# A trunk layer on eight cores: attention weights summed before the ones product, one bias added from PSUM, a revised planner, some Toeplitz pieces on ScalarE

## The reference

```python
x = x + 0.5 * swiglu_ffn(rmsnorm(x, ffn1_norm), ffn1_w_in, ffn1_w_out)      # D 1024, D_FF 2816
h = rmsnorm(x, mix_norm)
u_conv, q, k, v, g_conv, g_attn = jnp.split(h @ w_in, idx, axis=-1)
a = conformer_conv(u_conv, ...)        # GLU, causal depthwise width 31, layernorm, silu, projection
b = sliding_window_gqa(q, k, v, ...)   # 16 query heads, 4 key heads of 64, window 128
merged = jax.nn.sigmoid(g_conv) * a + jax.nn.sigmoid(g_attn) * b
x = x + merged @ w_out
x = x + 0.5 * swiglu_ffn(rmsnorm(x, ffn2_norm), ffn2_w_in, ffn2_w_out)

# inside the attention, per block of 128 queries and its two key blocks
s = s + bias[None, None]
m = jnp.maximum(jnp.max(s, axis=-1, keepdims=True), sink)
p = jnp.exp(s - m)
p = p / (jnp.sum(p, axis=-1, keepdims=True) + jnp.exp(sink - m))
o = jnp.einsum("bnhgqk,bnkhd->bnqhgd", p, vw)
```

## Time and profile before

| what | value |
|---|---|
| median of three executions | 3040.81 us |
| the profiled execution's own time | 3036.41 us |
| its span, slowest core (core 7) | 3034.8 us |
| spans of all cores | 3018.6 to 3034.8 us |
| PE busy, core 7 | 2973.1 us, 98% |
| DVE, ACT, POOL busy, core 7 | 1236.7, 836.3, 743.4 us |

### The profile page before, as it was taken

One profiled execution on the slowest core, in us unless ns is written; L12 is line 12 of the kernel. 1 busy time (PEld: TensorE's weight loads), 2 busy tenths in 40 slices (PEclk: granted clock), 3 DMA queues, 4 the chain that ended last, 5 costly groups with the idle time before them and its releaser, 6 DMA issues.

```text
span 3034.8 us, 41593 instructions; the slowest of 8 cores (3018.6 to 3034.8 us)
## 1 busy us (share of the span) xinstructions
PE 2973.1 (98%) x14660; PEld 1340.0 (44%) x14660; DVE 1236.7 (41%) x1700; ACT 836.3 (28%) x1482; POOL 743.4 (24%) x655
## 2 busy tenths in 40 slices
PE   6999999999999999999899999999999999999998
PEld 3444444444444454454334434434444444444443
DVE  4323345423344223757444454553323333223333
ACT  4111123211123222414666656642211111111110
POOL 3100012100003434293465555563000000000000
PEclk9999999999999999999999999999999999999999
DMA  7514249513148677967934545689442139332102
GB/s 181 92 23 70 35 115 239 105 21 60 21 100 218 133 181 174 221 121 231 179 81 138 143 140 149 161 194 237 138 90 42 21 69 228 87 63 35 18 1 111
DMA packets 330440, 354.09 MB, mean 117 GB/s; under 512 B 228352, under 2 KB 230400, under 8 KB 330240
## 3 DMA queue, kind: packets, MB, share of 16 engines
q1 hardware_dynamic: 295104, 252.82, 29.7%
q0 software_dynamic: 35136, 98.62, 20.4%
HBM read 294.79 MB, written 117.44 MB: 136 GB/s over the span
## 4 chain that ended last, share of the span: by engine, by line
PE 91%; DMA 3%; DVE 2%; SPq 1%; issue 1%; ACT 1%; POOL 1%; DVEq 0%; ACTq 0%; POOLq 0%
PE ps L480 91%; DMA zsh<-z_s 1%; SPq L513 1%; DMA z_s<-zfm 1%; DVE bst L828 1%; DMA sg<-sig_s 1%; DVE y L836 0%; DMA x<-x 0%; DVE y L838 0%; SPq L516 0%; ACT rs L501 0%; DMA hA<-xn 0%; POOL pt L959 0%; ACT tfM L501 0%; ACT et L501 0%
## 5 line engine op out<-in xcount | busy, mean ns | idle before, releaser
L480 PE MATMUL ps<-hA,wup 128*128 128x512 bf16 x5632 | 1226.7, 379 | 1.4 <-DVE sg L999 0.7
L480 PEld LDWEIGHTS ps<-hA,wup 128*128 128x128 bf16 x5632 | 551.1, 98 | 667.0 <-issue 5.7
L480 PE MATMUL ps<-wdn,hid 128*128 128x512 bf16 x2768 | 605.0, 379 | 0.0
L501 ACT ACTIVATE tfA<-ps 128x512 f32<-128x512 f32 x352 | 209.8, 597 | 1432.9 <-PE ps L480 1430.6
L644 DVE TENSOR_TENSOR hid<-ps,tfA 128x512 bf16<-128x512 f32 x346 | 238.9, 691 | 878.2 <-PE ps L480 867.4
L658 DVE SCALAR_TENSOR_TENSOR x<-ps,x 128x512 f32<-128x512 f32 x512 | 351.4, 690 | 228.9 <-PE ps L480 228.6
L480 PEld LDWEIGHTS ps<-wdn,hid 128*128 128x128 bf16 x2768 | 270.7, 98 | 326.7 <-issue 0.3
L959 POOL TENSOR_TENSOR pt<-et,EB 128x1024 bf16<-128x1024 bf16 x126 | 270.2, 2167 | 136.4 <-ACT et L501 135.0
L480 PE MATMUL ps<-hB,wG 128*128 128x512 bf16 x1024 | 229.2, 379 | 0.0
L480 PE MATMUL ps<-hB,wS 128*128 128x512 bf16 x1024 | 224.0, 379 | 0.0
L501 ACT ACTIVATE tfB<-ps 128x512 f32<-128x512 f32 x192 | 112.0, 595 | 318.8 <-PE ps L480 267.0
(11 more groups left out here) (79 smaller groups left out, 1817.1 us busy)
## 6 DMA issues: line engine op xcount, KB each, us to landing
x<-x SPq DMA_DIRECT2D x96, 512.0 KB, 7.8
sig_s<-tfB SPq DMA_DIRECT2D x128, 256.0 KB, 5.0
sg<-sig_s SPq DMA_DIRECT2D x128, 256.0 KB, 3.6
wup<-w1u POOLq DMA_DIRECT2D x44, 512.0 KB, 6.8
wup<-w2u POOLq DMA_DIRECT2D x44, 512.0 KB, 7.4
xM<-x SPq DMA_DIRECT2D x32, 512.0 KB, 5.6
x<-xM SPq DMA_DIRECT2D x32, 512.0 KB, 5.0
out<-x SPq DMA_DIRECT2D x32, 512.0 KB, 3.6
```

What stands on the lines that cost most here:

```text
L480: inst = e.matmul(o, l, r, start=st, stop=sp)
L501: return e.activation(**kw)
```

## The change

It does the following.

1. In `att`, the scores of both roles are one operation (four matmuls in a row, four banks at once). For role 0 the bias itself, not its exponential, is added on VectorE from PSUM (`sb`), and ScalarE writes the exponential of that straight to `pt`; role 1 goes through `et` and the POOL product as before. When there are two roles, POOL adds the two weight tiles (`psm`), and one pair of `ones` matmuls on that sum takes the place of two pairs. `et` and `psm` have one buffer each. The exponentials of `EB` 0 and 2 are no longer taken.
2. `att(0, n)` for p = 0 is placed between the parts of `qkv(0)`.
3. In the second half of the convolution, every other Toeplitz piece is built by ScalarE in 8 small operations (128 of them in all) and not by POOL.
4. At the start of `ffn("a")`, the loads of up-weights 2 to 5 wait for the first four normalised blocks; in the order of POOL the first one now comes after the first block's `rstd`, and weights 2 to 5 after the seventh block's.
5. The planner's rates of DMA, some costs (z transfers, `glu`, `ln`), the VectorE preference (layernorm 300 numbers later) and the ScalarE table rule change, and norm scalars get tokens of their own. So every engine's order is new nearly everywhere.
6. The last tile has its own `cact` buffer, `ffn("c")` uses its `hA` buffers in another order, and the last store is split in two.

The core of the diff:

```diff
-DMA_GBPS = 0.25e6
+DMA_GBPS = {"sp": 0.38e6, "pool": 0.24e6}
...
+            if e == "dve":
+                pick = min(now, key=lambda i: i + (300 if ops[i].tag == "ln" else 0))
             if e == "act":
                 need = ops[pick].table
-                if need is not None and need != table:
+                if need is not None and need != table and t - wait[e][pick] < 5.0:
...
             got = load_x(0, 0)
-            w = [load_up(f0)]
-            for f in range(f0 + 1, f1):
-                w.append(load_up(f, got[-1:]))
+            w = [load_up(f0, got[:1]), load_up(f0 + 1, got[3:4])]
             load_x(0, 1)
+            make_h_pe(0)
+            for f in range(f0 + 2, f1):
+                w.append(load_up(f, [normed[0]]))
...
+            if s == 1 and G % 2:
+                for ch in range(8):
+                    ov = tp.v(f=lambda a, ch=ch: a.rearrange("p g b (r c) -> p c (g b r)", c=8)[:, ch, :])
+                    P.add("act", lambda e, ov=ov, G=G, ch=ch: e.activation(out=ov.ap, in_=kk[c % 2].t[:, 192 * G:192 * G + 192], func=AF.Copy,
+                                                                       scale=cmaskf.t[:, ch:ch + 1]), [kk[c % 2].v(), cmaskf.v()], [tp.v()], 0.29, tag="toep")
...
+            todo = [(role, (blk - 1 + role) % 8, bank(2, keep=2)) for role in roles]
+            last_s = mm([PS(bs) for _, _, bs in todo],
...
+                for i in range(2):
+                    b_ = sbr.next()
+                    bias = EB[2 * p + role].v(slice(T * i, T * i + T))
+                    dve(lambda e, v=PS(bs, i), b_=b_, bias=bias: e.tensor_tensor(out=b_.t[:], in0=v.ap, in1=bias.ap, op=ALU.add),
+                        [PS(bs, i), bias], [b_.v()], T, tag="bias")
+                    act(p_.v(i), b_.v(), AF.Exp, T, tag="exp")
...
+            if len(made) == 2:
+                sum_ = psr.next()
+                pool(lambda e, a=made[0][2], b=made[1][2], sum_=sum_: e.tensor_tensor(
+                    out=sum_.t[:].rearrange("p a n -> p (a n)"), in0=a.t[:].rearrange("p a n -> p (a n)"),
+                    in1=b.t[:].rearrange("p a n -> p (a n)"), op=ALU.add), [made[0][2].v(), made[1][2].v()], [sum_.v()], 2.2, tag="psum")
...
+                for i in range(2):
+                    out.append((ps[64 * i:64 * i + 64, bo.banks[1], :], ones.t[:], sum_.t[:, i, :], True, True))
...
-    qkv(0, [8, 0, 1, 2, 3, 10, 9, 4, 5, 6, 7, 11, 12, 13])
+    qkv(0, [8, 0, 1, 2, 3, 10])
+    for n in range(4):
+        att(0, n, [0])
+        qkv(0, [[9, 4, 11], [5, 12], [6, 13], [7]][n])
```

More of the change, by code:

```diff
@@ L424, in build @@
     rs = [buf("rs%d" % i, 163 + 2 * i, [T], F32) for i in range(3)]
-    et = [buf("et%d" % i, 169 + 2 * i, [2, T], BF16) for i in range(2)]
+    sb = [buf("sb%d" % i, 169 + 2 * i, [T], F32) for i in range(2)]
     pt = [buf("pt%d" % i, 173 + 2 * i, [2, T], BF16) for i in range(4)]
-    tfM = [buf("tfM%d" % i, 182 + 2 * i, [T], F32) for i in range(4)]
+    tfM = [buf("tfM%d" % i, 182 + 2 * i, [T], F32) for i in range(2)]
+    et = [buf("et%d" % i, 186, [2, T], BF16) for i in range(1)]
+    psm = [buf("psm%d" % i, 188, [2, T], BF16) for i in range(1)]
     sg = [buf("sg%d" % i, 132 + 2 * i, [T], F32) for i in range(6)]
@@ L433, in build @@
     wO = [buf("wO%d" % i, 40 + 4 * i, [2, D], BF16) for i in range(4)]
-    cact = buf("cact", 56, [KC, T], BF16)
+    cacts = [buf("cact%d" % i, [56, 88][i], [KC, T], BF16) for i in range(2)]
     mg = buf("mg", 64, [KC, T], BF16)
@@ L664, in finish @@
                 xt = xb[4 * i + tb]
+                if xn_dst is None and (s, i, tb) == (1, 3, 3):
+                    for hf in range(2):
+                        c = slice(512 * hf, 512 * hf + 512)
+                        dma("sp", "x%d" % (12 + hf), x_dst[r0:r0 + 128, c], xt.t[:, c], [xt.v(c)], [(dst_tok, r0 // 128, hf)], 128 * D * 2)
+                    continue
                 dma("sp", "x%d" % (4 * i + tb), x_dst[r0:r0 + 128, :], xt.t[:], [xt.v()], [(dst_tok, r0 // 128)], 128 * D * 4)
@@ L722, in ffn @@
                         load_x(0, i, [last[0]])
-                        if i == 0:
-                            hold = [last[0]]
                     up(i, f0 + 1, f1, hd, 1)
+                    if s == 0 and q == 0 and i == 0:
+                        hold = [last[0]]
                     if pend is not None:
@@ L889, in build @@
             if step == ("gate", 0, 7):
-                for j in range(4):
+                for j in (1, 3):
                     act(EB[j].v(), EB[j].v(), AF.Exp, D)
@@ new lines, in att @@
+            todo = [(role, (blk - 1 + role) % 8, bank(2, keep=2)) for role in roles]
+            last_s = mm([PS(bs) for _, _, bs in todo],
+                        lambda todo=todo, p=p: [
+                            (ps[:, bs.banks[i], :], kn.t[64 * i:64 * i + 64, p, ks, :],
+                             qn.t[64 * i:64 * i + 64, 4 * p:4 * p + 4, 128 * n:128 * n + 128], True, True) for _, ks, bs in todo for i in range(2)],
+                        [kn.v(p, ks) for _, ks, _ in todo] + [qn.v(slice(4 * p, 4 * p + 4), slice(128 * n, 128 * n + 128))],
+                        0.15 + 0.216 * len(todo), tag="scores")
@@ new lines, in att, with mms @@
+            if len(made) == 2:
[3 more added lines that the diff above has]
+                    in1=b.t[:].rearrange("p a n -> p (a n)"), op=ALU.add), [made[0][2].v(), made[1][2].v()], [sum_.v()], 2.2, tag="psum")
+            else:
+                sum_ = made[0][2]
+            def mms(bo=bo, made=made, sum_=sum_, p=p):
+                out = []
+                for role, ks, p_ in made:
+                    for i in range(2):
+                        out.append((ps[64 * i:64 * i + 64, bo.banks[0], :], vb.t[:, ks, 64 * (2 * p + i):64 * (2 * p + i) + 64], p_.t[:, i, :],
+                                    role == roles[0], role == roles[-1]))
+                for i in range(2):
+                    out.append((ps[64 * i:64 * i + 64, bo.banks[1], :], ones.t[:], sum_.t[:, i, :], True, True))
+                return out
@@ L974, in att @@
+            mm([PS(bo)], mms, [m[2].v() for m in made] + [vb.v(m[1]) for m in made] + [sum_.v(), ones.v()], 0.13 + 0.216 * (1 + len(made)),
+               tag="av", after=[last_s])
             d_ = tfMr.next()
@@ L986, in merge @@
     def merge(t, fcs):
-        o = ob[t % 2]
+        o, cact = ob[t % 2], cacts[t == NT - 1]
         for fc in fcs:
@@ L1035, in load_cact @@
     def load_cact(t):
-        load_tr("cact", cact, cact_d, t * T, [("cact", t // 4, r) for r in range(16)], tag="cact")
+        load_tr("cact%d" % (t == NT - 1), cacts[t == NT - 1], cact_d, t * T, [("cact", t // 4, r) for r in range(16)], tag="cact")
     for j in range(2):
```

105 lines of the change are left out of this document (50 added, 55 removed).

## The result

The changed kernel took 3122.08 us (median of 4 runs, 3119.13 upward) beside 3038.28 us for the kernel before: a ratio of 1.0277, 95% interval 1.0254 to 1.0301. That is slower by over 2%, to which the prediction gave 0.02. In some executions the cores of one die run at a lower granted clock and take longer; medians are over all executions, ratios leave these out, so kernels are compared by their ratios.

A forecast was written before the change was run, and what follows sets the result against it. TensorE, busy 98% of the span, was taken as the bound: 3036.4 - 29.2 + 2 - 4 + 7.7 - 2 - 3 - 1 - 1 = 3005.9 us, forecast as 3007, range 2986 to 3028.

The forecast's parts named there:

- part 6: Convolution stage and tail: ScalarE's small Toeplitz operations at 0.35 us each, 45 us in all, hidden: zero, up to +5 us.
- Part 1: TensorE's work in attention: -29.2 us, 13.4 from fewer `ones` pairs and 15.8 from 158 fewer shape changes.
- Part 2: Steady attention, chain from scores to `av`: 6.0 us, covered by TensorE work except one tight place; +2 us, 0 to +20.
- a longer chain: Rival: queueing on POOL stretches a unit's chain in attention to 8 us, six tiles lose 12 us; 3023 us, chance 0.14.
- VectorE blocking POOL: Rival: VectorE's bias adds hold up POOL in attention, chain 9.5 us, slower than before; 3071 us, chance 0.06.
- Part 3: Entry into attention: `sq` wait goes (-4 us), POOL-fed units at the end of t = 0 wait 11.8 us; net +7.7.
- Part 4: Exit from attention: POOL's weight load still waits for transposes, but TensorE has more cover; -2 us, from -6 to +8.
- Part 5: Start: no weight-load issues before the fourth block's `rstd`, first product before 25 us; -3 us, from -7 to +3.
- Part 6's other terms: Convolution's DRAM round trips -1 us through better prices, and two half stores at the end -1 us.

The follow-up runs named there:

- run 2: The kernel before with only the Toeplitz change (every other piece of the second half built by ScalarE): 3129.54 us, ratio 1.0297.
- run 3: The changed kernel with its 128 ScalarE operations writing 192 adjacent values each, so the convolution's coefficients are misplaced: 3060.14 us, ratio 1.0039.
- run 5: The kernel before with only the new attention (`att`, its buffers and the two `EB` exponentials): 3021.33 us, ratio 0.9944.
- run 12: The changed kernel with all Toeplitz pieces on POOL, both DMA rates 0.25, VectorE and `glu` repriced, and no interleaved `att(0)` visits: 3011.37 us, ratio 0.9894.
- run 7: The changed kernel with all Toeplitz pieces on POOL and both planner DMA rates back at 0.25: 3029.47 us, ratio 0.9944.
- run 1: The changed kernel with all Toeplitz pieces built by POOL again, all else kept: 3033.14 us, ratio 0.9988 to the kernel before.

## Why the prediction was wrong

**The step that failed is part 6: the price of the ScalarE operations.** It put 192 columns between one column and 512, at 0.35 us, and called ScalarE mostly idle, "zero, up to +5". Measured: 1.156 us each (run 2: 1.158), and 89 us in all. The row used as the upper end, 0.60 us, is of a contiguous output, and the lower one, 0.20 us, of a single column. Run 3 shows that the interpolation had been somewhat low even for a contiguous output (0.453), and that the 16-byte step of the store makes the other 0.70. A row of another access pattern bounds nothing; that was the mistake, and the range inherited it.

**What it cost can be worked out from the view that was not opened.** TensorE's products on the last 32 pieces took 101 us before, with ScalarE busy 18.2. In the changed kernel 15 of ScalarE's 16 pieces fall into that stretch. They bring 15 x 8 x 1.156 = 138.7 us: together 156.9, 56 more than there is. (Neighbouring operations overlap a little; ScalarE was busy 149.5 us.) The rest of the 81 us by which the stretch grew is time in which ScalarE still stood idle, 182 - 149.5 = 32.5 us: 14.6 until TensorE finished a product for `tfB`, 7.0 until it gave a piece's buffer back, and gaps too short to be listed. No row of before gives that part. At 0.453 us the pieces bring 54.4, together 72.5 of 101: it fits, and yet run 3 kept 13 to 20 us of waits, for pieces that each come a little late. The point from which ScalarE is full is an estimate from the same rows: (101 - 18.2) / 120 = 0.69 us an operation.

**"A late piece would hold TensorE about 2.8 us at a time."** The mechanism was named and sized by the same wrong price: eight operations are 9.2 us, and the waits are about 7 us at most places. What the sentence left out is the clock: behind nine of the ten waits the first 12 matmuls run at 1.2 GHz.

The Trainium skill (ScalarE: Activation LUTs, What ACT_TABLE_LOAD costs) gives 186 ns, 93 ns for a pointer operand and 0.833 ns a column, which for 192 columns makes an estimate of 439 ns; run 3's 453 agrees, run 2's 1158 does not. The Trainium skill (SBUF — State Buffer, Door 1) has what was missing: SBUF has 16-byte lines, and an access that crosses to a new one pays a penalty. Here every value does. The 0.70 us agrees with that in kind; no run here varies the step otherwise, so the line size is the page's, not shown.

**Part 1 (-29.2 us of TensorE work): right.** 128 `ones` matmuls, and 26 to 29 us off the span without waits in run 5. The split, 13.4 and 15.8, came out as some 10 and 16 to 19, the second by subtraction.

**Part 2 (chain 6.0 us, +2): right.** The sum 2.17 us, the add 0.68, no steady wait for POOL, 1.8 us idle in 415 in run 5. In the changed kernel VectorE's `sb` holds TensorE 5.2 us between 1640 and 2040 us, where +2 was taken. The two rivals on a longer chain and on VectorE blocking POOL are out: `pt` took 2.15 us beside the adds.

**Part 3 (entry +7.7): mechanism right, releaser wrong.** The wait for `sq` is gone, from 4.75 us to at most 1.8. At the end of t = 0 four waits of 1.75, 1.50, 2.51 and 2.51 us and one of 0.77 make 9.0 us against 11.8, but they end on VectorE (`sb`, `o`) and not on POOL. Before the visits at 1615.18 and 1620.15 us POOL's sum had ended 0.8 and 0.3 us earlier, `o` of the unit before, which reads PSUM, only 0.14 us earlier. So the chain through POOL was nearly as long as the wait, and the one from `ones` over the sink, Ln and Exp to `o`, which the prediction didn't count, was a little longer. That interleaving buys nothing, as the net sum said, is what run 12 shows.

**Part 4 (exit -2): wrong sign.** The weight load of POOL waits 5.0 us for a transpose and TensorE 3.16 us behind it, and just behind the attention `sg` costs 7.9 us, where the kernel before waited 3.2 for it in all; run 5 has the same wait, 8.9 us. **Part 5 (start -3): right** at its row, 24.64 against 27.87 us, but the waits for `xnA` fall from 23.0 only to 20.2. **Part 6's other terms:** `zsh` from 6.1 to 3.7 us, more than the 1 said; the last matmul ends 8.8 us before the end of the span and not 9.2, so the half stores gave 0.4 us of 1. Not in the sum: `tfA`, 9.9 us, from the rates, run 7.

Without the pieces the sum would have been 3006 against 3033 measured (run 1), 27 us too low: 13 us are the rates, and the rest is, as far as the tables of waits show, waits that came where others went, as `sg` at the exit did (8.6 us in run 1).

## What to carry to other kernels

Before work is moved to an idle engine, open the window into which it will fall, divide the free time of that engine by the number of operations, and ask whether the price can lie above the quotient; here it was 0.69 us, with 0.35 assumed and 1.16 true. Below the quotient single pieces can still come late: at 0.453 us 13 to 20 us of waits stayed. Take a price only from a row with the same access pattern, the output's step included; if there is none, the upper end is open. When TensorE is the bound, a wait can cost more than its own length: here the work behind the waits of 3.7 to 7.5 us ran at the lower clock. Compare the span without waits, too.

## What the runs showed of the hardware

A ScalarE scaled copy of 128 x 192 bf16 takes 1156 ns when its outputs are 16 bytes apart and 453 ns when they lie side by side: 3.7 ns more a value. The POOL product that does the whole piece with 1536 contiguous outputs takes 2746 to 2753 ns, so the eight small operations, 9.2 us, are over three times dearer in engine time than what they replace. A bf16 sum on POOL of 128 x 1024 costs what a product does (2169 and 2149 ns). In the stage with ten waits, most of 7 us, TensorE's granted clock was 0.84, against 1.00 without them, and the span without waits was 19 us longer.
